# Sums of squares split into two fp32r passes, and a reordered gating stage with a late-scaled first output tile

## The reference

```
h = rmsnorm(x, g);  proj = h @ w_in
u, z_ssm, q, k, v, z_att, f_pre = split(proj)
# S5 branch (scan over u, gelu -> zs)
y_ssm = zs * sigmoid(zs @ w_glu + b_glu) * silu(z_ssm)
y_ssm = rmsnorm(y_ssm, ssm_ng)
# attention branch: 8 heads of 128
q = rmsnorm(q per head, qg);  k = rmsnorm(k per head, kg)
o = softmax(q k / sqrt(128) + forget sums, causal) v
y_att = rmsnorm(o * silu(z_att), att_ng)
out = x + concat(y_ssm, y_att) @ w_out
```

## Time and profile before

| | us |
|---|---|
| median of 3 runs (2173.99 to 2178.43) | 2177.96 |
| the profiled execution | 2175.9 |
| its span, first to last instruction | 2174.3 |
| PE busy in the span | 2055.3 (95%) |
| DVE busy | 973.6 (45%) |
| ACT busy | 708.2 (33%) |
| POOL busy | 519.3 (24%) |
| one head in the steady state | 124.2 |
| gating stage, 1600.5 to 1740.45 | 139.95 |
| output chunk 0, 1740.45 to 1786.86 | 46.41 |

### The profile page before, as it was taken

The page is one execution under the profiler, slowest core; times in us unless marked ns, Lnnn a source line. Parts: engine busy times, 40 slices in busy tenths (PEclk is TensorE's granted clock), DMA queues, the critical chain, the costliest instruction groups (busy, mean ns, idle before and its releaser), DMA issues.

```text
span 2174.3 us, 36318 instructions
## 1 busy us (share of the span) xinstructions
PE 2055.3 (95%) x12932; PEld 1966.9 (90%) x12932; DVE 973.6 (45%) x1795; ACT 708.2 (33%) x1458; POOL 519.3 (24%) x771
## 2 busy tenths in 40 slices
PE   4789999999969999999999999999999889999997
PEld 3579999999969999999999999999988879999997
DVE  6454555555533334342524444352564553333332
ACT  5413332333333233333333333334365531111110
POOL 6964555444500001010010101001022212222222
PEclk8799999999989999999999999999999989999999
DMA  6222222222122212112121212112173533333222
GB/s 189 45 68 65 69 69 58 59 69 69 51 57 57 62 32 80 33 43 70 33 81 31 81 31 76 36 44 68 47 265 114 154 98 85 91 87 90 82 84 56
DMA packets 194779, 162.17 MB, mean 75 GB/s; under 512 B 26755, under 2 KB 176429, under 8 KB 193381
## 3 DMA queue, kind: packets, MB, share of 16 engines
q1 hardware_dynamic: 163984, 97.89, 17.2%
q0 software_dynamic: 14704, 51.19, 7.8%
q10 hardware_dynamic: 16036, 12.39, 1.8%
HBM read 124.47 MB, written 36.95 MB: 74 GB/s over the span
## 4 chain that ended last, share of the span: by engine, by line
PE 65%; DMA 2%; DVE 2%; issue 1%; ACT 1%; POOL 0%; SPq 0%; DVEq 0%; POOLq 0%; ACTq 0%
PE GB L188 46%; PE TB L188 9%; PE TB L1781 3%; PE TB L1802 3%; PE TB L1843 1%; PE TB L1826 1%; PE TB L1898 1%; PE TB L1858 1%; DMA ys_s<-QR 1%; DVE QR L1538 0%; DVE QR L1536 0%; DMA out_k_sample<-KO 0%; DMA XL<-ys_s 0%; ACT whi L172 0%; DMA KO<-zs_s 0%
## 5 line engine op out<-in xcount | busy, mean ns | idle before, releaser
L188 PE MATMUL GB<-XH,whi 128*128 128x384 f32 (+1 forms) x2880 | 970.4, 337 | 28.6 <-DVE wlo L176 16.7
L188 PE MATMUL GB<-XH,wlo 128*128 128x384 f32 (+1 forms) x2880 | 947.7, 329 | 0.0
L188 PE MATMUL GB<-XL,whi 128*128 128x384 f32 (+1 forms) x2880 | 945.1, 328 | 0.0
L176 DVE TENSOR_TENSOR wlo<-wraw,whi 128x256 fp32r<-128x256 f32 x544 | 265.9, 490 | 830.1 <-ACT whi L172 826.5
L188 PEld LDWEIGHTS GB<-XH,whi 128*128 128x128 f32 x2880 | 545.8, 190 | 45.0 <-issue 23.6
L188 PEld LDWEIGHTS GB<-XL,whi 128*128 128x128 f32 x2880 | 545.9, 190 | 0.0
L188 PEld LDWEIGHTS GB<-XH,wlo 128*128 128x128 f32 x2880 | 544.7, 189 | 0.0
L172 ACT CAST whi<-wraw 128x256 fp32r<-128x256 f32 x544 | 219.5, 405 | 992.3 <-PE GB L188 811.7
L1247 POOL DMA_DIRECT2D ya_s<-ZR x7 | 4.1, 579 | 750.7 <-DVE ZR L1610 750.7
L1637 DVE RECIPROCAL SQ<-SQ 128x136 f32<-128x136 f32 x128 | 127.7, 997 | 1.1
L188 PE MATMUL TB<-XH,wlo 128*128 128x384 f32 (+1 forms) x384 | 126.0, 328 | 0.0
(11 more groups left out here) (389 smaller groups left out, 2182.7 us busy)
## 6 DMA issues: line engine op xcount, KB each, us to landing
wraw<-in_w_in SPq DMA_DIRECT2D x384, 128.0 KB, 2.2
wraw<-in_w_out SPq DMA_DIRECT2D x128, 128.0 KB, 2.2
xt<-in_x_prompt SPq DMA_DIRECT2D x5, 1024.0 KB, 5.0
NCB<-nc_s POOLq DMA_DIRECT2D x8, 608.0 KB, 5.3
zg_s<-U ACTq DMA_DIRECT2D x8, 544.0 KB, 2.8
XL<-zg_s SPq DMA_DIRECT2D x8, 544.0 KB, 4.6
VR<-zg_s POOLq DMA_DIRECT2D x8, 544.0 KB, 4.6
KO<-zs_s POOLq DMA_DIRECT2D x8, 544.0 KB, 5.9
```

What stands on the lines that cost most here:

```text
L176: V.tensor_tensor(wlo[:, s % SPL], wraw[:, s % RAW], whi[:, s % SPL].bitcast(f32), ALU.subtract).then_inc(self.lo, 1)
L188: ins = T.matmul(group(GB if bank is None else bank, b), w[:, s % SPL, kk], x[:, k + kk, c:c + n], start=first and kk == 0 and i == 0, sto ...
```

## The change

1. In a head, ACT's square goes in fp32r into a new tile `SQH`; DVE squares the same values in fp32 into `SQ` and subtracts `SQH`, which gives `SQL` (in the place of `SQ`). PE multiplies `SQH` by ones in fp32r, waits for `SQL`, and accumulates that product on top. These six matmuls stand right behind the step's weight piece, ahead of its attention output matmuls, and their 64-column part lands in another bank, so the wait for `y` is gone.
2. In the gating stage DVE's gate comes ahead of its `split_lo`; POOL issues the store of the gated tile ahead of the next two loads; the running sum of squares is added on DVE (`add_squares`) one step after the gate; the splits of the attention outputs stand at a step's end and at other steps.
3. In chunk 0 the splits of the S5 half are spread over steps 0 to 4; the first attention half is copied out of PSUM unscaled and scaled later (`scale_att`); the broadcasts stand after steps 5 and 7, both into `GB`, straight from the column of norms, without a diagonal made by DVE.

```diff
-            YA_AT = {1: 0, 4: 1, 6: 2, 9: 3, 11: 4, 14: 5, 17: 6, 29: 7}
-            SUM_AT, SCALE_AT, ROOT_AT, BC_AT = {0: 1, 4: 0}, {4: 0}, {4: 0}, {2: 1, 6: 0}
-            TR_AT = 2
+            YA_AT = {1: 0, 9: 1, 14: 2, 17: 3, 20: 4, 22: 5, 25: 6, 29: 7}
+            YS_AT = {0: (0, 1), 2: (2, 3), 3: (4, 5), 4: (6, 7)}
+            SUM_AT, SCALE_AT, BC_AT = {0: 1, 4: 0}, {1: 1, 5: 0}, {5: 1, 7: 0}
+            TR_AT, BC_AT_ATT = 2, 5
...
                         if n == 0:
                             pool.wait_ge(e["v_mm"], NH)
                             pool.wait_ge(e["k_out"], 32 * NH)
                         else:
-                            pool.wait_ge(e["yg"], n)
+                            finish_glu(n - 1)
                         pool.dma_start(ZG[:], zg_s[n * P:(n + 1) * P, :]).then_inc(e["zs_in"], 16)
                         pool.dma_start(ZS, zs_s[n * P:(n + 1) * P, :]).then_inc(e["zs_in"], 16)
-                        if n:
-                            finish_glu(n - 1)
...
                                 if w:
-                                    act.wait_ge(e["qn_r"], h + 1)
+                                    act.wait_ge(e["ss_mm"], 2 * h + 1)
                                 elif att:
-                                    act.wait_ge(e["kn"], h)
-                                    act.wait_ge(e["sqa"], ha)
-                                S.activation(SQ[:], raw[:], ACT.Square).then_inc(e["sq"], 1)
+                                    act.wait_ge(e["v_mm"], h)
+                                S.activation(SQH[:], raw[:], ACT.Square).then_inc(e["sq"], 1)
...
+                            if gemm and s in SQ_AT:
+                                w, raw = SQ_AT[s]
+                                dve.wait_ge(e["ga"], 9 * h + 2 * w + 2)
+                                dve.wait_ge(e["gd"], 3 * h + w + 1)
...
+                                V.tensor_tensor(SQ[:], raw[:], raw[:], ALU.mult).then_inc(e["sqf"], 1)
+                                dve.wait_ge(e["sq"], 2 * h + w + 1)
+                                dve.wait_ge(e["sqf"], 2 * h + w + 1)
+                                V.tensor_tensor(SQL[:], SQ[:], SQH[:].bitcast(f32), ALU.subtract).then_inc(e["sql"], 1)
...
+                                for c, d, n in parts:
+                                    T.matmul(TB[:, d:d + n], onesr[:], SQH[:, c:c + n], start=True, stop=False)
+                                pe.wait_ge(e["sql"], 2 * h + w + 1)
+                                for c, d, n in parts:
+                                    ins = T.matmul(TB[:, d:d + n], onesr[:], SQL[:, c:c + n], start=False, stop=True)
+                                ins.then_inc(e["ss_mm"], 1)
...
-                                for c, d, n in ((0, 0, 512), (512, 512, 512), (SEQ, 4 * 512 + P, DEC)):
-                                    ins = T.matmul(TB[:, d:d + n], ones[:], SQ[:, c:c + n], start=True, stop=True)
-                                ins.then_inc(e["ss_mm"], 1)
...
                         dve.wait_ge(W.mm, W.multiplied(out_piece(n, HPC - 1)))
-                        if isinstance(n, int) and n == 0:
-                            dve.wait_ge(f["bc"], 3)
                         for (src, dst), (_, r) in zip(halves(GB, OT[b]), halves(GB, RB[1])):
-                            V.tensor_tensor(dst, src, r, ALU.mult).then_inc(f["ea"], 1)
+                            if isinstance(n, int) and n == 0:
+                                V.tensor_copy(dst, src).then_inc(f["ea"], 1)
+                            else:
+                                V.tensor_tensor(dst, src, r, ALU.mult).then_inc(f["ea"], 1)
...
+                    def scale_att(b):
+
+                        dve.wait_ge(f["bc"], 3)
+                        dve.wait_ge(f["ea"], 2)
+                        V.tensor_tensor(OT[b][:], OT[b][:], RB[1][:], ALU.mult).then_inc(f["sa"], 1)
```

More of the change, by code:

```diff
@@ L1092, in build_kernel @@
         free_semaphores()
+        with ExitStack() as st:
+            SQL = st.enter_context(nc.sbuf_tensor("SQL", [P, TOK], r32))
         SQ, SQA = sb("SQ", [P, TOK]), sb("SQA", [P, TOK])
@@ L1097, in build_kernel @@
             sbp = pool_of(st)
-            QR, KR, VR, ZR = (sbp(n, [P, TOK]) for n in ("QR", "KR", "VR", "ZR"))
+            QR, KR = (sbp(n, [P, TOK]) for n in ("QR", "KR"))
+            with ExitStack() as over:
+                SQH = over.enter_context(nc.sbuf_tensor("SQH", [P, TOK], r32))
+            VR, ZR = (sbp(n, [P, TOK]) for n in ("VR", "ZR"))
+            onesr = sbp("onesr", [P, P], r32)
             QN, KN = sbp("QN", [P, TOK]), sbp("KN", [P, TOK])
@@ L1381, in part @@
                                     split_z(k)
-                            if not gemm and s in YA_AT:
-                                split_ya(YA_AT[s])
                             if not gemm and s % GP == GP - 1:
@@ L1472, in part @@
                                 S.copy(KO[0:DEC, TT - 1], TB[0:DEC, 4 * 512:4 * 512 + P]).then_inc(e["k_act"], 1)
+                            if not gemm and s in YA_AT:
+                                split_ya(YA_AT[s])
                             if not gemm and s % GP == GP - 2:
@@ L1513, in out_chunk @@
                                 W.split_hi(m, s + SPL, (OUT0 + s + SPL) // RAW + n * (NPO // RAW) + 1)
-                            if first and s in ROOT_AT:
-                                root(ROOT_AT[s])
+                            if first and s in YS_AT:
+                                for k in YS_AT[s]:
+                                    split_ys(k)
+                            if first and s in SCALE_AT:
+                                root(SCALE_AT[s])
+                                if SCALE_AT[s]:
+                                    square_glu(KG - 1)
                             if first and s in BC_AT:
@@ L1587, in part @@
                                     rest_z(k)
-                            if not gemm and s in YA_AT:
-                                rest_ya(YA_AT[s])
+                            if not gemm and s % GP == 0 and s:
+                                gate_glu(s // GP - 1)
                             if gemm and s in (7, 15, 23):
@@ L1637, in part @@
                                         o.then(V.reciprocal(a, a))
+                            if not gemm and s in YA_AT:
+                                rest_ya(YA_AT[s])
                             if gemm and s == QN_AT:
@@ L1660, in scales @@
                         sums = TB[:, 4 * 512 + TT * w:4 * 512 + TT * (w + 1)]
-                        tiles = ((slice(0, P), slice(0, TT - 1)), (slice(0, DEC), slice(TT - 1, TT)))
-                        ms, rt, rr, tmp = (lambda p, m, i=i: rm[p, i, w, m] for i in range(4))
-                        for p, m in tiles:
-                            ins = V.tensor_scalar(ms(p, m), sums[p, m], 1.0 / D_SSM, EPS, ALU.mult, ALU.add)
-                        ins.then_inc(f["ms"], 1)
-                        dve.wait_ge(f["rt"], 2 - w)
@@ L1675, in scales @@
-                        V.tensor_scalar(DG[w][0:DEC, SEQ:], ident[0:DEC, 0:DEC], rm[0:DEC, 2, w, TT - 1:TT], None, ALU.mult
-                                        ).then_inc(f["dg"], 1)
+                        ms, rt, rr, tmp = (rm[:, i, w] for i in range(4))
+                        V.tensor_scalar(ms, sums, 1.0 / D_SSM, EPS, ALU.mult, ALU.add).then_inc(f["ms"], 1)
+                        dve.wait_ge(f["rt"], 2 - w)
+                        o.then(V.reciprocal(rr, rt))
+                        o.then(V.tensor_tensor(tmp, rr, rr, ALU.mult))
@@ L1721, in out_chunk @@
                                 W.split_lo(out_piece(n, s + SPL), s + SPL)
+                            if first and s in YS_AT:
+                                for k in YS_AT[s]:
+                                    rest_ys(k)
                             if first and s in SCALE_AT:
                                 scales(SCALE_AT[s])
+                                if SCALE_AT[s]:
+                                    add_squares(KG - 1)
+                            if first and s == BC_AT_ATT + 1:
+                                scale_att(b)
                             if not first and s == TR_AT:
```

106 lines of the change are left out of this document (49 added, 57 removed).

## The result

| | before | after |
|---|---|---|
| median of 4 runs | 2177.52 (2173.99 to 2178.43) | 2137.03 (2135.31 to 2138.15) |
| the profiled execution | 2175.9 | 2138.15 |
| ratio of the times, 95% interval | | 0.9819 (0.9803 to 0.9834) |

A forecast was written before the change was run, and what follows sets the result against it. PE bounds the kernel, busy 2055.3 of 2174.3 us, so its work, gaps and clock count. Terms of 17.4 + 9.9 + 10.5 = 37.8 us off 2175.9 gave 2138.1 us, range 2125 to 2156.

The forecast's parts named there:

- Term 1: Heads, sums of squares at 16 places: cheaper fp32r matmuls and no wait for `y`; -17.4 us, between -20 and -11.
- the return: Heads, step 20: the first fp32r matmul after the fp32 ones takes 0.26 us instead of 0.17, costing 0.09 more.
- Term 2: Gating stage: shorter waits of PE for the sigmoids and one half-clock stretch gone; -9.9 us, between -3 and -14.
- the 3.59: Gating stage, PE's sigmoid wait at 1654.73: 1.2 us left; the half-clock stretch behind it, costing 1.7 us, should go.
- The 3.35 us at 1629.06 stay: Gating stage, first gate: PE's wait of 3.35 us remains, since the gate waits for loads the change doesn't move.
- Term 3: Chunk 0: -7.9 for the diagonal's wait, -4.2 for clock, +1.6 for a new wait; -10.5 us, between -6 and -14.
- The 3.3 us at 1747.4: Chunk 0: a half-clock stretch of 3.3 us behind the one-column sums, kept because those sums stay.
- (1): Gating stage keeps its waits in another form, through DVE's single queue; gain there shrinks to 2, 2146 us; chance 0.14.
- (2): Clock stays lower: new and remaining waits each bring 3.4 us at half clock, 3 times 1.7 us; 2143 us; chance 0.09.
- (3): Heads: low parts come some 0.9 us late at each of 16 places, 14 us in all; 2152 us; chance 0.08.
- (4): Heads: low parts so late the kernel gets slower, from 2.4 us per place; 2186 us at 3 us; chance 0.03.
- (5): Heads: an fp32r pass of ones costs what fp32 did, 42 us more; 2180 us; chance 0.04.

The follow-up runs named there:

- the gating part alone: The kernel before with only the gating stage's new order: median 2164.20 us, ratio 0.9939, gating stage 130.76 us.
- sums alone: The kernel before with only the split sums of squares in the heads, gating stage and chunk 0 as before: median 2161.76 us, ratio 0.9923.
- the doubled square: The changed kernel with one more DVE square, same values into the same tile, ahead of the low part at each of 16 places: 2154.65 us, ratio 0.9892.
- chunk 0 alone: The kernel before with only chunk 0's new order: median 2165.63 us, ratio 0.9943, chunk 0 35.42 us.
- gate back: The changed kernel with head 0's POOL copy late, the second broadcast after step 6 and two splits moved, first gate at its changed-kernel place: 2134.86 us, ratio 0.9806.

## Why the prediction was right, step by step

It said 2138.1 us, in 2125 to 2156; measured were 2137.03. Each of the three terms had the right sign and nearly the size, and the mechanisms stood, except for parts of the clock and for head 0. The closeness of the total is in part luck. The terms missed by 1.6, 2.1 and 1.9 us, in both directions: the three stages gave 40.2 us where 37.8 were forecast. In the profiled execution the 2.7 us ahead of the first head hide that, and against the medians it is hidden in part, since the forecast started from 2175.9, 1.6 us under the median 2177.52. Two sums of the text don't come out: the terms' bounds add up to -48 (2128), not to -51, and 124.2 less twice 0.83 and 0.65 is 121.9, not 121.7.

**Term 1, -17.4 forecast, -15.8 measured.** The price of a place, 1.12 us worked out, was 1.07. The 0.09 us of the return were credited wrongly, since they stay: behind the six fp32r matmuls too the first weight matmul takes 0.25 us until the next. So a place gains 0.79 us and not 0.83. "A head of 121.7 us" was 121.93. In heads 1 to 7 the gain is (974.26 - 104.32) - (958.48 - 104.75) = 16.2 us, and the working gives the same for them (14 times 0.83, and 4.6). The agreement is a little too good: six heads gained 2.22 us each, the last one 2.8, of which 0.5 is a longer last step in this one profile of the kernel before (4.41 us; 3.88 in both other profiles with the old sums). What was mis-sized most is head 0: forecast -1.7, measured +0.4. Its two steps with the sums went from 4.83 to 4.38 and from 4.83 to 5.30 us, in sum no gain. From the first high part to the first low one PE takes 0.79 us at step 9 and 1.72 at step 20, where it takes 0.49 in the other heads. So the low parts start 0.3 and 1.2 us late. Of the second, 0.9 is POOL's copy `QN`, which falls on a weight split of DVE: the case that the text foresaw for POOL in general and allowed 0.5 us for. The 0.3 are there at step 9 with no POOL instruction near, and at step 20 with the copy moved; DVE's pair stands behind its weight split in both. Another 0.4 is not the change's: half clock from the phase ahead reached 4.91 us into head 0 before and 5.79 us after, at half the work per us. First before, then after:

```profile
626.25:631.16 4.91, 4.91 (x16) 0.50 0.52 126
```

```profile
628.95:634.74 5.79, 5.79 (x19) 0.50 0.44 106
```

The prediction put each place where POOL meets DVE's new pair at "up to 2.5 us later". In head 0 the meeting costs 0.9 us, and it is the split in front of the pair that pays (1.35 against 0.43 us); with the copy moved PE's wait of 1.07 us is gone. The Trainium skill, SBUF — State Buffer, "Who interferes with whom", has the port pair that both use as an exclusive lock; the trace agrees in head 0, where the copy starts first. In the other heads no wait for `SQL` is left at all: PE has only one, of 1.1 us. The changed kernel's trace says why: in heads 1 to 7 no POOL instruction runs beside any square or subtraction of the 14 pairs. The copy stands elsewhere there (at 852.34, for one); in six of the seven heads it holds a weight split, for 1.31 to 1.33 us, and PE does not wait for that one.

**Term 2, -9.9 forecast, -12.0 measured.** The waits gave 7.8 of the 8.2 forecast: the second was left at 1.17 (forecast 1.2), the one ahead of chunk 0 at 1.07 (1.0), and the one at the first gate stayed (3.08 for 3.35). The one step that failed is the clock: I gave back 1.7 us, for the stretch behind the 3.59, and kept the first gate's ("The 3.35 us at 1629.06 stay", with "that gap and its clock too" only in the bound). The wait stayed, the profile after has no half clock, and 4.2 us came back. The 2.5 us more are no merit of the edits in this stage: with the same edits and the old heads the 6.8 us at half clock were there (the gating part alone). By the undone edits, the DVE add is worth 4.9 us in the stage and the early gate and store 5.3, with 2.6 more in chunk 0; the moved splits, to which I had given part of the 2.4 us, are worth nothing in sum. (Each is read from one profile; by the medians undoing them costs 6.0, 6.6 and 0.3 us.) The add's 4.9 holds 3.3 us of idle time and 1.6 of clock behind the first gate (PE busy 121.12 of 132.81 us):

```profile
1587.77:1720.58 132.81, 121.12 (x732) 0.99 0.50 172
```

3.3 and 5.3 us of waits make 8.6, near the 7.8 that the whole stage lost in idle time.

**Term 3, -10.5 forecast, -12.4 measured.** The 7.90 us wait went, the new one took 1.37 us (forecast 1.6). PE's busy time fell from 38.35 (38.51 in the earlier trace rows, whose window ends 0.16 us later) to 32.50, 5.85 us where I gave 4.2. It is the clock: the stretches at half clock of 5.00 and 3.30 us and this one of 3.40, right behind the 4.66 us wait, are worth half their sum, 5.85.

```profile
1740.50:1743.90 3.40, 3.40 (x11) 0.50 0.92 318
```

The step that failed is "The 3.3 us at 1747.4 follow the one-column sums, which stay, so I keep them". The sums stayed, but for the last one, which now takes 128 tokens and not 64, and the half clock went. All three profiles with the old chunk 0 (before, sums alone, gating alone) have a stretch of 3.4 us that begins 0.3 to 1.4 us behind the sums' end; none of the eleven with the new chunk 0 has. In the gating part alone no wait over 1.2 us and no half clock stands in the 100 us ahead of it, so there it came without a long wait, behind the sums. Why they don't in the new order, where they hold PE for 1.92 us and not for 1.97 to 1.98, stays open.

**The rivals.** (1), the gating waits in another form: only the first gate's wait is of that kind, and 7.8 of 8.2 us went. (2), a clock that stays lower: in the changed kernel no; in the gating part alone it did so, by 2.8 us in that stage. (3) and (4), low parts late: not at the 14 places of heads 1 to 7, at the two of head 0 by 0.3 and 1.2 us; the doubled square shows the mechanism at its full price. (5), fp32r as dear as fp32: refuted by 1.07 against 1.86 us, and by the 10.3 us that going back to fp32 costs.

## What to carry to other kernels

Where one engine is busy 95% of the time, cut the span at its own landmarks and compare stages, with idle and busy time apart: a difference of 1 us is then visible, where single executions scatter by 3. At constant work the change of a stage's busy time is its clock; look at it first, since it moved the gating stage by up to 2.8 us with the stage's own code unchanged. Before giving an engine new work whose result the bottleneck waits for, measure the slack at the place itself: here 0.28 us of it carried 15.8 us of gain, and one more instruction of 1.29 us ate all of that, with the engine still half idle. Take both-operand work of DVE and work of POOL out of each other's way, also where each alone is short.

## What was not expected of the hardware

The clock behind one and the same wait. Twelve of the profiles have the first gate at the same steps, and PE waits there, for `PR`, 2.33 to 3.85 us. Half clock then lasted 6.8 us in three of them (before; gating stage alone; chunk 0 alone), 3.4 us in four (sums alone; fp32 sums at their new place; add on POOL; gate back), and did not come in five (the changed kernel in both its profiles; the doubled square; gate and store late; splits at their old steps). That is 0 to 2.8 us of time: the 6.8 us begin within the wait, so that PE loses half of some 6. The five without had waits of 2.33 to 3.08, the four with 3.4 us waits of 3.04, 3.19, 3.74 and 3.85, the three with 6.8 waits of 3.12, 3.35 and 3.82: whether half clock comes goes nearly with the length here (3.04 and 3.08 the wrong way round), how long it stays does not, and elsewhere in the stage waits of 2.26 and 2.50 us had 3.4 us of it beside them. The three with 6.8 us are the three with the old sums of squares in the heads; what the link is, or whether it is one, stays open. A forecast should carry such a wait as a range. Rival (2)'s rule (the Trainium skill, TensorE: Matmul & The Clock Gate, "HAM oscillation — how this bites in real kernels") says that waits which are long enough bring half rate; here waits at one place did in seven profiles and not in five, and behind the one-column sums of the gating part alone half rate came without such a wait.

The length of a hold. In head 0 a split of 0.43 us took 1.35 beside POOL's copy of 1.10, and in the gating stage 3.40 beside POOL's add of 2.55: both times it ends 0.3 us behind the POOL instruction. They differ in the start. The copy starts first, by 0.02 us; the split beside the add is on record from 1630.76, 0.56 us ahead of the add at 1631.32, and alone it would have been done by then. What holds it until the add starts, while POOL issues a load, is not shown. A cheap instruction pays for a meeting as a dear one does: 2.97 us here, and 2.23 for the split of 1.35 us beside the same add.
